# Three places for gathered rows and four for table tiles, instead of four and three, in a hybrid encoder's expert layer

## The chip, the cores and the metric

The kernel runs on one core of a Trainium2 chip. The metric is the device time of one execution in microseconds. It took 4031.67 us in the median of three runs, which lay between 4027.1 and 4036.65 us.

## What is computed

The program is a two-layer encoder trunk on 256 tokens of width 2048, all in float32. Each layer first mixes tokens in four parallel branches (a 2-D Fourier transform, a state space model, grouped-query attention and a bidirectional RWKV-7) and then applies an expert layer that looks up single-neuron experts by product keys. Only the expert layer is touched here:

```
q   = (xc @ w_query)                                  # 8 heads
s1, i1 = top_k(scores of half 1, 16);  s2, i2 = top_k(scores of half 2, 16)
top_s, pos = top_k(s1[:, None] + s2[None, :], 16)     # 16 of 256 candidates per token and head
idx  = i1 * 128 + i2 at pos                           # of 16384 experts
gate = softmax(top_s)
act  = gelu(sum_d expert_u[idx] * xc)
out  = sum over heads and picks of gate * act * expert_v[idx]
```

So each token uses 128 rows of `expert_u` and 128 rows of `expert_v`, each row 2048 numbers (8 KB) long.

## The kernel before, in words

Each of the two turns of the layer loop runs the mixers, the RWKV part, the output projection with the query projection (`route`), and then `experts`, which is the place of the change.

`experts` treats the tokens in two ways. 160 of them (`DENSE`) are computed densely: TensorE multiplies the whole tables with them, tile by tile. There are 128 tiles (`TILES`) of the transposed `peer_u` (this document calls them the u tiles), each [128, 2048] float32, that is 1 MB, and then 128 tiles of `peer_v` (the v tiles), also 1 MB each. A u tile costs 16 products into one bank (L1672), ScalarE applies the GELU to them (L1789, L1791) into `W`, and a v tile costs 16 products (L1745) that add up over all 128 tiles in six banks. The other 96 tokens are served sparsely: in three sets of 32 tokens, 32 steps for `peer_u` and 32 for `peer_v` each, 192 gathers in all (`ROWS_IN`). One gather brings one row for each of the 128 partitions (32 tokens by 4 picks), so again 1 MB, in two halves of 512 KB that GpSimd issues as two indirect DMAs (L1629). VectorE then takes it in `serve(n)`: a dot product for `peer_u` (L1935), a multiply-add into `sums` for `peer_v` (L1941).

Both streams have a ring of places in SBUF, and a place of either ring is 8 KB per partition. `ring` has `SLOTS` places for table tiles. SyncE issues tile i (L1593 for u, L1598 for v) when the products of tile i - SLOTS are done (semaphore `tile_mm`). The first `SLOTS` u tiles are issued without a wait, right behind the last piece of the query weights. `place` has `RING` places for gathered rows. GpSimd issues row n when VectorE has served row n - RING (semaphore `place_free`). The tiles go through the hardware queue q1, the gathers through the software queue q0; both use the same 16 DMA engines.

The order of VectorE's work is written out by hand. While TensorE goes through u tiles 0 to 61, VectorE looks for the best picks of the dense tokens (`find(0, h)`) and serves two rows after each head, and then serves on up to row 29. It then waits until u tile 60, since `exps(0)` stands there on ScalarE. From u tile 64 (`FIRST`) on it makes one-hot tables for the gates of four tokens per tile, multiplies gates into `W`, and serves 9 rows for every 10 tiles (`served`). TensorE makes the gates (L1681) ahead of tiles 64 to 103. With the v tiles VectorE has nothing but the remaining rows: it serves them as they come. TensorE puts a few small products among the tiles: `widen` (L1695) spreads a set's tokens for the dot products, `fold` (L1708) adds a set's sums up. After the last v tile TensorE folds the third set, which needs the sums of row 191, and transposes the dense results (L1761); VectorE adds both to `x` (L1950, L2009), and the layer is over.

In the following, four stages of `experts` are told apart. Their times in the second layer are: A1, u tiles 0 to 61 (2801 to 3086 us); A2, the u tiles with gates, 62 to 103 (3086 to 3302 us); A3, the remaining u tiles (3302 to 3419 us); V, the v tiles (3419 to 4012 us). In the first layer they begin at 787, 1072, 1288 and 1409 us, and V ends at about 2002 us.

Of the kernel before, what the change touches and what calls it, by code (L numbers as in the profile page):

```python
# [32 lines left out]
HALF_K = 8  # L33
WRING = 3
TILES = KEYS
SLOTS = 3
RING = 4
SET, SETS, STEPS = 32, 3, 32
DENSE = SEQ - SET * SETS
ROWS_IN = SETS * 2 * STEPS  # L40
# [81 lines left out]
def build(nc, t, out):  # L122
# [3 lines left out]
    with whole:  # L126
        first_sem = []

        def sem(name):
            s = whole.enter_context(nc.semaphore(name))  # L130
            first_sem.append(s)
            return s
# [35 lines left out]

        row_in = [sem(f"row_in{i}") for i in range(RING)]
        kept = len(first_sem)  # L170
# [1237 lines left out]
def query_piece(nc, t, layer, query, engine, h):  # L1408

    engine.dma_start(query["w"][:, h % WRING], t["peer_w_query"][layer][:, h * P:(h + 1) * P]  # L1410
                     .rearrange("(k p) n -> p k n", p=P)).then_inc(query["w_in"][h % WRING], 16)
# [118 lines left out]
def experts(nc, t, layer, sem, sb, bank, c, x, hT, query, W, low, layer_base, row_in):  # L1530
# [8 lines left out]
    rms_wide, rms_mm, h_scaled = sem("ex_rms_wide"), sem("ex_rms_mm"), sem("ex_h_scaled")  # L1539
    tile_in, tile_mm, tile_out = [sem(f"ex_tile_in{i}") for i in range(SLOTS)], sem("ex_tile_mm"), sem("ex_tile_out")  # L1540
    best_ready, exp_ready, picks_ready, picks_mm, picks_out = [sem("ex_" + n) for n in ("best", "exp", "picks", "picks_mm",
# [7 lines left out]
    with ExitStack() as st:  # L1549
# [3 lines left out]

        ring = sb(st, "ex_tile", [P, SLOTS, KT * P])
        place = sb(st, "ex_row", [P, RING, D])
        h_wide = sb(st, "ex_h_wide", [P, D])
# [30 lines left out]
        with nc.Block() as block:  # L1587
            @block.sync
            def _(sp):
                def u_tile(i, slot, free):  # L1590
                    if free is not None:
                        sp.wait_ge(tile_mm, free)
                    sp.dma_start(ring[:, slot, :], t["peer_uT"][layer, i].rearrange("p k e -> p (k e)"))\  # L1593
                        .then_inc(tile_in[slot], 16)
# [6 lines left out]
                for h in range(WRING, PEER_H):  # L1601
                    sp.wait_ge(q_mm, h - WRING + 1)
                    query_piece(nc, t, layer, query, sp, h)
                whole_laps = TILES // SLOTS
                for i in range(SLOTS):
                    u_tile(i, i, None)
                with sp.Fori(1, whole_laps) as lap:
                    for e in range(SLOTS):
                        u_tile(lap * SLOTS + e, e, lap * SLOTS + (e + 1 - SLOTS))
                for i in range(whole_laps * SLOTS, TILES):  # L1610
# [11 lines left out]
            def _(pool):  # L1622
                pool.wait_ge(rows_ready, SETS * 4 * 2)
                for n in range(ROWS_IN):
                    s, table, step = n // (2 * STEPS), n // STEPS % 2, n % STEPS
                    if n >= RING:
                        pool.wait_ge(place_free, n - RING + 1)
                    for half in range(2):
                        nc.gpsimd.indirect_dma_start(  # L1629
                            out=place[:, n % RING, half * D // 2:(half + 1) * D // 2], out_offset=None,  # L1630
                            in_=tables[table][:, :],
                            in_offset=bass.IndirectOffsetOnAxis(ap=rows[:, s, half, step:step + 1], axis=0))\
                            .then_inc(row_in[n % RING], 16)

# [400 lines left out]
```

## Time and profile before

| | us |
|---|---|
| median of three runs | 4031.67 |
| the profiled execution, its own time | 4039.34 |
| its span, first to last instruction | 4037.5 |
| TensorE busy in the span | 3754.7 |
| VectorE busy in the span | 2310.8 |
| GpSimd busy in the span | 977.3 |
| moved by the DMA engines | 1077.47 MB |

The profile is of one execution. Busy time is the union of an engine's instructions; issues of DMAs on SyncE are not counted as busy, while those of GpSimd (the indirect ones) are. "DMA share" in a window is the mean busy share of the 16 DMA engines; it can come out slightly above 1. In the chain of waits a piece "DMA" is the time from a DMA's issue to its landing, when that landing is what released the next piece.

### The profile page before, as it was taken

To read this page: it belongs to the slowest core of one execution; us is meant where nothing else is said; L and a number is where in the kernel's file an instruction comes from. 1 tells how busy PE (TensorE), PEld (TensorE's weight loads), DVE (VectorE), ACT (ScalarE), POOL (GpSimd) and SP (SyncE) were. 2 spreads that over 40 slices of the span, in tenths; PEclk is the share of its full clock that TensorE was granted. 3 is DMA by queue.
4 is the path that set the end of the run, shared out by engine and by line. 5 is a ranking of instruction groups with operands and counts; after the bars stand their busy time and mean duration, and the time that the engine had idled before them with its cause. 6 is when DMAs were issued, how large, how long until landed. Compare 5 with 4: busy or idle time off the path is not lost. (4 is left out here: it accounts for less than half of the span.)

```text
span 4037.5 us, 63918 instructions
## 1 busy us (share of the span) xinstructions
PE 3754.7 (93%) x26660; PEld 3402.6 (84%) x26660; DVE 2310.8 (57%) x4099; ACT 429.9 (11%) x1020; POOL 977.3 (24%) x868
## 2 busy tenths in 40 slices
PE   6997889999999999999869978899999999999997
PEld 5776774899999999999857867748999999999997
DVE  6975752695287534344469757527952875444444
ACT  1013220100111000000010132101001110000000
POOL 2510000034033333333226100000340333333331
PEclk9998899999999999999989988999999999999999
DMA  5340014399799999999744300153997999999997
GB/s 155 117 133 10 1 43 155 123 358 402 277 381 381 414 416 414 415 412 415 317 127 132 118 10 1 43 161 126 369 409 282 380 386 412 415 415 415 412 414 305
DMA packets 334771, 1077.47 MB, mean 267 GB/s; under 512 B 52197, under 2 KB 150873, under 8 KB 268441
## 3 DMA queue, kind: packets, MB, share of 16 engines
q1 hardware_dynamic: 223896, 670.72, 43.8%
q0 software_dynamic: 110592, 402.70, 25.2%
q8 instruction: 212, 3.47, 0.4%
q14 instruction: 71, 0.57, 0.0%
HBM read 1071.23 MB, written 2.10 MB: 266 GB/s over the span
## 5 line engine op out<-in xcount | busy, mean ns | idle before, releaser
L1745 PE MATMUL bank<-ex_W,ex_tile 128*128 128x160 f32 x8192 | 1132.6, 300 | 39.1 <-DMA ex_tile<-in_peer_v 38.8
L1745 PEld LDWEIGHTS bank<-ex_W,ex_tile 128*128 128x128 f32 x8192 | 1114.9, 190 | 60.3 <-DMA ex_tile<-in_peer_v 52.9
L1672 PE MATMUL bank<-ycT,ex_tile 128*128 128x160 f32 x8192 | 1142.8, 300 | 24.0 <-DMA ex_tile<-in_peer_uT 21.7
L1672 PEld LDWEIGHTS bank<-ycT,ex_tile 128*128 128x128 f32 x8192 | 1119.3, 190 | 39.9 <-DMA ex_tile<-in_peer_uT 30.5
L1629 POOL DMA_INDIRECT ex_row<-in_peer_u,ex_rows x384 | 404.1, 1052 | 1850.9 <-DVE ex_rows L1905 1188.7
L1941 DVE SCALAR_TENSOR_TENSOR ex_sums<-ex_row,ex_weight,ex_sums 128x2048 f32<-128x2048 f32 x186 | 437.0, 2349 | 411.4 <-DMA ex_row<-in_peer_v,ex_rows 362.3
L1935 DVE CUSTOM_DVE_ANT_0 ex_row<-ex_row,ex_h_wide 128x2048 f32<-128x2048 f32 x192 | 438.7, 2290 | 366.7 <-DMA ex_row<-in_peer_u,ex_rows 288.9
L1629 POOL DMA_INDIRECT ex_row<-in_peer_v,ex_rows x384 | 364.7, 950 | 890.2 <-DVE ex_sums L1941 560.5
L359 PE MATMUL pj_bank<-pj_hT,pj_piece 128*128 128x256 f32 x2048 | 459.5, 383 | 5.9 <-DVE pj_hT L632 3.6
L359 PEld LDWEIGHTS pj_bank<-pj_hT,pj_piece 128*128 128x128 f32 x2048 | 388.4, 192 | 72.0 <-issue 13.8
L824 PE MATMUL bank<-arena,ycT 128*128 128x512 f32 x512 | 222.4, 593 | 2.0 <-PEq L909 2.0
L824 PEld LDWEIGHTS bank<-arena,ycT 128*128 128x128 f32 x512 | 96.6, 190 | 121.4 <-issue 121.2
L994 PE MATMUL bank<-arena 128*128 128x128 f32 x1152 | 140.9, 283 | 7.6 <-DVE arena L1342 7.5
L994 PEld LDWEIGHTS bank<-arena 128*128 128x128 f32 x1152 | 136.7, 198 | 10.3 <-issue 10.1
L1993 DVE TENSOR_TENSOR ex_W<-ex_W,ex_gelu 128x160 f32<-128x160 f32 (+26 forms) x128 | 35.2, 275 | 174.7 <-ACT ex_gelu L1789 97.2
L1417 PE MATMUL bank<-ycT,query_w 128*128 128x256 f32 x512 | 114.9, 382 | 2.0 <-PEq L1434 2.0
L1791 ACT ACTIVATE ex_W<-bank 128x160 f32<-128x160 f32 (+20 forms) x206 | 57.0, 277 | 525.1 <-PE bank L1672 480.3
L1417 PEld LDWEIGHTS bank<-ycT,query_w 128*128 128x128 f32 x512 | 95.8, 190 | 16.5 <-issue 2.7
L1919 DVE TENSOR_SCALAR ex_hot<-consts,ex_picksT 128x128 f32<-128x128 f32 x320 | 109.5, 342 | 0.0
L1516 DVE TENSOR_TENSOR x<-bank,x 128x512 f32<-128x512 f32 x16 | 11.1, 692 | 168.3 <-PE bank L824 168.1
L1918 DVE TENSOR_SCALAR ex_hot<-consts,ex_picksT 128x128 f32<-128x128 f32 x320 | 90.2, 282 | 15.4 <-ACT ex_picksT L1823 15.4
L605 POOL TENSOR_TENSOR s_table<-s_factor 128x1024 f32<-128x1024 f32 x16 | 32.6, 2035 | 273.8 <-DVE s_factor L710 151.2
(375 smaller groups left out, 3129.3 us busy)
## 6 DMA issues: line engine op xcount, KB each, us to landing
ex_tile<-in_peer_uT SPq DMA_DIRECT2D x256, 1024.0 KB
ex_tile<-in_peer_v SPq DMA_DIRECT2D x256, 1024.0 KB
pj_piece<-in_w_in SPq DMA_DIRECT2D x32, 2048.0 KB, 8.8
arena<-in_w_out SPq DMA_DIRECT2D x16, 2048.0 KB, 8.2
query_w<-in_peer_w_query SPq DMA_DIRECT2D x16, 1024.0 KB, 6.0
ex_row<-in_peer_u,ex_rows POOLq DMA_INDIRECT x384
ex_row<-in_peer_v,ex_rows POOLq DMA_INDIRECT x384
x<-in_x SPq DMA_DIRECT2D x1, 2048.0 KB, 8.8
```

What stands on the lines that cost most here:

```text
L359: mm = mmul(pj_bank[:, n % 2, m * SEQ:m * SEQ + SEQ], piece[:, n % 2, k, m * P:m * P + P], hT[:, k, :], start=(m == 0 and k == 0), stop=(k ...
L824: mm = nc.tensor.matmul(bank[:, out_bank(n) + b, :], ycT[:, kh * HALF_K + k, b * P:b * P + P], out_w["place"][:, i % 2, k, :], start=(kh = ...
L994: mm = mmul(bank[:, b, j * P:j * P + P], left[:, d, j, :], right[:, d, j, :], start=(j == 0), stop=True, skip_group_check=True)
L1417: mm = nc.tensor.matmul(bank[:, h % 2, 0:SEQ], query["w"][:, h % WRING, k, :], hT[k // 4][:, k % 4, :], start=(k == 0), stop=(k == KT - 1) ...
L1629: nc.gpsimd.indirect_dma_start(out=place[:, n % RING, half * D // 2:(half + 1) * D // 2], out_offset=None, in_=tables[table][:, :], in_off ...
L1672: mm = mmul(o, ring[:, j % SLOTS, k * P:k * P + P], hT[k // 4][:, k % 4, 0:DENSE], start=(k == 0), stop=(k == KT - 1))
L1745: mm = mmul(bank[:, at_, lo:lo + DENSE], ring[:, i % SLOTS, m * P:m * P + P], W[:, j, :], start=(j == 0 and m % 3 == 0), stop=(j == TILES ...
L1791: last = A.activation(W[:, j, n:DENSE], a[:, n:DENSE], ACT.Gelu)
L1918: V.tensor_scalar(hot2[:, g % 2, i, :], c("iota"), picksT[:, 1, n:n + 1], None, ALU.is_equal)
L1919: mm = V.tensor_scalar(hot1[:, g % 2, i, :], c("iota"), picksT[:, 0, n:n + 1], picksT[:, 2, n:n + 1], ALU.is_equal, ALU.mult)
L1935: V.tensor_tensor_reduce(out=row, in0=row, in1=h_wide[:], scale=1.0, scalar=0.0, op0=ALU.mult, op1=ALU.add, accum_out=dot[:, step:step + 1 ...
L1941: V.scalar_tensor_tensor(sums[:], row, weight[:, step:step + 1], sums[:], ALU.mult, ALU.add)\
```

## The change

Two constants are exchanged. `SLOTS` becomes 4 and `RING` 3. All else follows from them: the places of the two rings (`ring` and `place`), the number of their semaphores, the waits that free a place (`i - SLOTS`, `n - RING`), and the way SyncE's two loops over the tiles are split into whole turns and a rest. With `SLOTS` = 4 the loops come out even: 128 tiles are 32 turns of four.

```diff
--- before.py
+++ after.py
@@ -33,8 +33,8 @@
 HALF_K = 8
 WRING = 3
 TILES = KEYS
-SLOTS = 3
-RING = 4
+SLOTS = 4
+RING = 3
 SET, SETS, STEPS = 32, 3, 32
 DENSE = SEQ - SET * SETS
 ROWS_IN = SETS * 2 * STEPS
```

## Rows read from the trace of the kernel before

**Rows 1.** The page: DMA share and GB/s in 40 slices, then the two queues

```profile
DMA  5340014399799999999744300153997999999997
GB/s 155 117 133 10 1 43 155 123 358 402 277 381 381 414 416 414 415 412 415 317 127 132 118 10 1 43 161 126 369 409 282 380 386 412 415 415 415 412 414 305
q1 hardware_dynamic: 223896, 670.72, 43.8%
q0 software_dynamic: 110592, 402.70, 25.2%
```

**Rows 2.** Busy times by stretch: stages of layer two, three stretches inside, V of layer one

```profile
core 0: us, PE busy (x) PEld busy (x) DVE busy (x) ACT busy (x) POOL busy (x), PEclk, DMA share, GB/s
2801.00:3086.00 285.00, 275.57 (x2011) 272.51 (x2011) 172.06 (x461) 31.07 (x79) 83.26 (x68) 1.00 0.90 351
3086.00:3302.00 216.00, 216.00 (x1648) 215.68 (x1648) 173.56 (x434) 31.81 (x129) 62.32 (x67) 1.00 0.92 355
3302.00:3419.00 117.00, 114.76 (x812) 109.53 (x812) 60.45 (x75) 7.83 (x27) 43.27 (x45) 1.00 1.02 411
3419.00:4012.00 593.00, 571.72 (x4127) 560.02 (x4125) 248.44 (x155) 8.06 (x17) 193.97 (x206) 1.00 1.01 410
...
3033.00:3086.00 53.00, 52.69 (x387) 52.45 (x387) 0.78 (x3) 6.45 (x15) 0.00 (x0) 1.00 0.77 286
3640.00:3780.00 140.00, 135.13 (x981) 133.20 (x980) 55.37 (x45) 0.00 (x0) 46.01 (x49) 1.00 1.02 415
```

**Rows 3.** TensorE's waits for tiles: A1, A3, V, each layer one and then two

```profile
PE bank L1672 <- DMA ex_tile<-in_peer_uT: 9.2, 10, 3.9
...
PE bank L1672 <- DMA ex_tile<-in_peer_uT: 8.1, 8, 3.1
...
PE bank L1672 <- DMA ex_tile<-in_peer_uT: 2.4, 4, 1.1
...
PE bank L1672 <- DMA ex_tile<-in_peer_uT: 2.0, 3, 0.9
...
PE bank L1745 <- DMA ex_tile<-in_peer_v: 19.7, 30, 1.1
...
PE bank L1745 <- DMA ex_tile<-in_peer_v: 19.1, 27, 1.2
```

**Rows 4.** Chain of waits in A1: start us, us, what

```profile
2882.86 9.47 DMA ex_tile<-in_peer_uT
2892.34 0.04 issue
2892.38 8.97 PE bank L1672 x64
```

**Rows 5.** Chain of waits in V, one turn of a row's place, and a shorter flight

```profile
3760.57 19.46 DMA ex_row<-in_peer_u,ex_rows
...
3780.06 2.29 DVE ex_row L1935
3782.35 0.02 DVE ex_dot L1935
3782.37 0.26 issue
3782.63 0.94 POOL ex_row L1629
3783.56 0.30 issue
...
3810.60 14.73 DMA ex_row<-in_peer_u,ex_rows
```

**Rows 6.** Timeline at the end of V: last tiles, last rows, then fold

```profile
3989.59 22.00 PE L1745 MATMUL bank<-ex_W,ex_tile 128*128 128x160 f32 x160 [0.89 <-DMA ex_tile<-in_peer_v]
...
4007.05 4.84 DVE L1941 SCALAR_TENSOR_TENSOR ex_sums<-ex_row,ex_weight,ex_sums 128x2048 f32<-128x2048 f32 x2 [2.89 <-DMA ex_row<-in_peer_v,ex_rows]
...
4012.00 3.80 PE L1708 MATMUL bank<-ex_sums,consts 128*32 128x512 f32 x8 [0.41 <-DVEq L1945]
```

**Rows 7.** Timeline of VectorE: row 29 served, and the wait for ScalarE behind it

```profile
3025.23 2.29 DVE L1935 CUSTOM_DVE_ANT_0 ex_row<-ex_row,ex_h_wide 128x2048 f32<-128x2048 f32 x1 [4.29 <-DMA ex_row<-in_peer_u,ex_rows]
...
3079.04 0.29 DVE L1890 TENSOR_REDUCE ex_total<-ex_picks 128x8 f32<-128x128 f32 x1 [51.50 <-ACT ex_picks L1796]
```

**Rows 8.** The page: a 1 MB load while no other stream runs, us to landing

```profile
query_w<-in_peer_w_query SPq DMA_DIRECT2D x16, 1024.0 KB, 6.0
```

## The prediction

> **What bounds the kernel now.** I read the slices of the page first: outside `experts` the DMA engines are half idle, inside it they are nearly always full at about 415 GB/s, and their two queues move two thirds of all bytes there [rows 1]. Then the windows by stage [rows 2]. In A1 TensorE is busy 275.6 of 285 us and the DMA engines 0.90; in A2 TensorE is busy all the time (its products alone set the pace) at 355 GB/s; in A3 and V the DMA engines are full (1.02 and 1.01) and TensorE loses 2 and 21 us. Third, who TensorE waits for: table tiles, 8 to 9 us in A1, 2 us in A3 and some 20 us in V in each layer [rows 3]. Last, the end of V [rows 6]: the last tile's products end at 3989.6 + 22.0 = 4011.6 us and the last row is served at 4007.05 + 4.84 = 4011.9 us. The two streams end together, and the fold behind them needs both. So V is bound by the volume that both streams put through the same 16 engines: 593 us at 410 GB/s are 243 MB, that is 232 pieces of 1.049 MB, which is about 128 tiles and the 105 rows that are left of 192 (87 are served by u tile 127, by `served`).
>
> That is the main point. **A place given to the other stream adds no bandwidth.** It can only win where the DMA engines have room now, and it can lose where one stream alone must fill them.
>
> **Where room exists, A1.** TensorE waits there for tiles though the mean load is 0.90. A tile is issued when the tile three before it is done, so it has two tiles' time, 8.97 us (the x64 are two tiles) [rows 4], and took 9.47 us. With four places it has three tiles' time, about 13.3 us. The longest wait is 3.9 us [rows 3], which is below the added 4.4 us. So all tile waits of A1 go: 9.2 + 8.1 = 17.3 us, 8.65 per layer. They are on the path: TensorE is what sets A1's length, and A2 behind it is TensorE's alone. What could be late next is VectorE with one row place fewer. Its row 29 is served at 3027.5 us, and then it waits 51.5 us for ScalarE [rows 7]. The 30 rows could each be 1.7 us later before that is used up. I cost it at nothing. The volume moved ahead in that pause is unchanged: the rings hold four tiles and three rows then instead of three and four. The pause runs at 286 GB/s in 53 us [rows 2], and it is what the 8.65 us are taken from.
>
> **A2.** No tile waits now, none after. A row is due every 5.24 us (a tile with its gates; 216 us for 40 such tiles and two without gates comes to about that). With three places a turn has 15.7 us. Of a turn, serving, release and first issue take 2.29 + 0.02 + 0.26 + 0.94 + 0.30 = 3.8 us [rows 5], so the flight may take 11.9 us. The trace does not show flights there, since none is waited for. In V, with the engines full, they take 14.7 to 19.5 us [rows 5], but most of that is queueing behind the stream's own other rows: 593 us for 105 rows are 5.65 us a row, and four places turn in 22.6 us. At 355 GB/s there is room, so I cost A2 at nothing; the third rival has it otherwise.
>
> **A3 and V, the tiles.** Here the 20 and 2 us of waits hang on the same rule, flight against two or three tiles' time. The longest wait is 1.2 us [rows 3], well inside the added 4.4. TensorE's V is then 571.7 us instead of 593 [rows 2], and with A1 and A3 its last tile ends 8.65 + 2.2 + 20.5 = about 31.4 us earlier in each layer. These 22.7 us of A3 and V are no gain in themselves, because the rows are not there.
>
> Whether the tiles can take more of the engines than now is the open step. The trace has both shares while both streams wait: 135.1 us of TensorE's 140 are busy, that is 30.6 tiles, and 49 half rows in the same 140 us [rows 2]. That is 229 GB/s for tiles and 184 for rows. A table tile goes as 8 KB packets and a row as 4 KB ones (402.70 MB in 110592 packets are 3.6 KB in the mean, the small ones are completions [rows 1]; a partition's share of a tile is 8 KB). The Trainium skill, page "DMA: Bandwidth & Descriptors", section on arbitration, says that an engine goes round robin between its queues, a packet at a time. By that rule two queues that are both never empty would share 2:1, 277 and 138 GB/s; the trace's 229 and 184 are between that and halves. If the rule holds, the tile queue is empty part of the time, and one more tile in flight fills it; if it does not, the shares stay. The sum below takes neither figure.
>
> I take it that the waits go, since TensorE cannot take more than a tile per 4.41 us: 238 GB/s. The rows then get 415 - 238 = 177 GB/s, 5.92 us a row instead of 5.65, and they are behind when the tiles are through.
>
> **The tail of V.** The last tile landed at about 4007.2 us (22.0 us of five tiles, less one, from 3989.6). After the change it lands 31.4 us earlier and another 4.4 us ahead of its use, about 3971. The last row is landed at about 4009.5 us now, and with the engines full throughout it would be 8.65 us earlier, 4000.8. So 29.5 us of full engines are left for rows alone: 29.5 x 415 / 1.049 = 11.7 rows. They must go through three places. A turn is 3.8 us plus the flight of a half row on free engines. The nearest row is the 1 MB load without a rival, 6.0 us [rows 8]; half of its bytes less (0.5 MB at 415 GB/s, 1.26 us) gives 4.7. (3.8 + 4.7) / 3 = 2.9 us a row, against 2.53 at full engines. 11.7 x 2.9 = 33.9 us, and the row stream ends at 4005.1, 4.3 us earlier than now. The bounds: VectorE with the release takes 2.6 us a row, which gives 30.4 us and 7.8 us earlier; a flight as long as that of a loaded tile, 9.47 us [rows 4], gives 4.4 us a row, 51.5 us and 13 us later. I take 2.9, because nothing competes in the tail. The fold and what follows it wait for the rows alone, as now.
>
> **Loss of fill.** With one row fewer in flight the engines might run empty between. A3 speaks against it: VectorE is paced by the tiles there, so rows often lie landed in their places, and the engines are still at 1.02 [rows 2]. Nothing for the sum.
>
> **Sum.** 4.3 us per layer, 8.6 us in all: 4039.3 of the profiled execution becomes 4030.7. The median of the runs is 0.19% below that execution, and in the same ratio I get 4031.7 - 8.6 = 4023 us. The bounds of the tail alone make it 4016 to 4058.
>
> **Rivals.**
> 1. *The shares are fixed by the queues.* Then a fourth place does nothing in A3 and V, tiles and rows end together as before, and A1's 17.3 us are all kept: 4014 us. For it: tiles fly over 9 us in A1 and in V alike. Against it: where TensorE is slower for the folds, the row flight falls to 14.7 us [rows 5], so the rows take what the tiles leave.
> 2. *Nothing moves.* If the tiles' flight grows with one more in the queue (their share being fixed already in A1), the waits of A1 stay too: 4032 us.
> 3. *The rows starve, the slower side.* Three places bear the forecast's 5.92 us a row as long as the flight is under 3 x 5.92 - 3.8 = 14 us; this is the deciding point. If it does not fall below the shortest one seen, 14.7 us, a row takes 6.2 us. While the tiles run (563 us) 91 rows are served instead of 95, four more are left for the tail at 2.9 us: 12 us per layer worse than the forecast, 7.5 us worse than now, 4047 us. The same flight breaks A2's 11.9 us: 6.2 x 0.9 = 5.6 us a tile against 5.24, up to 13.6 us over 40 tiles, of which VectorE's pauses (173.6 of 216 us busy [rows 2]) take part: up to 4074. Were the flight to stay at 18.7 us, a row would take 7.5 us and the time would pass 4130; but that needs the flight not to depend on the rows in front, which the four-place turn speaks against.
>
> **How the numbers follow.** Forecast 0.55, rival 1 0.15, rival 2 0.10, rival 3 0.20. A measurement of this kernel can tell about 0.2%, 8 us, from no change; the forecast's 8.6 us are on that edge, so of its 0.55 I put 0.29 to faster, 0.20 to the same and 0.06 to slower (a long tail). Faster: 0.29 + 0.15 = 0.44. Same: 0.20 + 0.10 = 0.30. Slower: 0.06 + 0.20 = 0.26. The range reaches from below rival 1 to the middle of rival 3: 4009 to 4062 us. The forecast's own is 4016 to 4040.
>
> **What the profile after would show.** TensorE's waits for tiles in A1 gone (they were 17.3 us) and A2 starting 8 to 10 us earlier in each layer; in V TensorE at about 572 us, waiting at its end some 20 us or more for row 191, with rows alone on the engines in the last 30 us at under 415 GB/s; row flights of about 14 us in V. If instead tile waits of 20 us remain in V and both ends coincide, rival 1 was right. If VectorE waits for rows in A2, or TensorE waits there at all, it is rival 3. The prediction is wrong above all if the tail runs slower than 3.3 us a row, or if the rows lose more than 0.27 us each while the tiles run.

## The result

The changed kernel took 4059.09 us in the median of four runs (4052.73 to 4061.04), the kernel before 4032.7 us in four (4027.1 to 4036.65). The ratio is 1.0063, 95% interval 1.0048 to 1.0078: 0.63% slower, some 26 us, where 9 us less was forecast. The range of 4009 to 4062 us holds it, on its slower side. The profiled executions stand at 4060.33 against 4039.34 us, 21 us apart. Of the eleven executions of the last experiment's kernel, two took 8860.52 and 6779.49 us; no comparison below counts them.

The page of the changed kernel, its slices first (DMA share and GB/s, 40 slices), to be read beside [rows 1]:

```profile
DMA  5340015499899999999644300154998999999996
GB/s 154 117 133 10 1 43 161 135 369 409 320 379 389 408 416 414 413 376 416 251 126 135 115 9 2 43 161 152 378 411 320 381 390 399 416 413 415 371 416 256
```

In V of both layers there are now two holes: slices of 376 and 371 GB/s in the middle, and last slices of 251 and 256, where the kernel before had 412 to 416 throughout and last slices of 317 and 305 [rows 1].

TensorE's waits, all of the execution that concern `experts`:

```profile
PE bank L1708 <- DVE x L1950: 56.3, 4, 24.5
PE bank L1708 <- DVEq L1945: 47.2, 2, 24.8
```

No wait for a tile is left, in any stage; those of [rows 3] are gone. In their place TensorE waits for VectorE, and so for the rows, at the folds (L1708): 103.5 us in the two layers.

Windows of layer two (A1, A3, V as a whole; then V cut into four parts, and two pieces of the second part; columns as in [rows 2]):

```profile
2809.00:3081.00 272.00, 272.00 (x2009) 271.74 (x2009) 171.91 (x461) 30.76 (x78) 75.23 (x66) 1.00 0.92 363
...
3297.00:3417.00 120.00, 115.73 (x818) 110.83 (x817) 58.77 (x73) 7.89 (x27) 40.06 (x43) 0.99 1.01 400
3417.00:4031.00 614.00, 565.00 (x4122) 559.85 (x4120) 250.50 (x157) 8.16 (x17) 215.57 (x210) 0.96 0.99 396
3417.00:3786.00 369.00, 369.00 (x2708) 366.98 (x2707) 141.31 (x92) 4.94 (x10) 114.63 (x123) 1.00 1.02 414
3786.00:3811.00 25.00, 0.50 (x5) 0.29 (x4) 14.49 (x13) 0.00 (x0) 16.15 (x12) 0.60 0.84 299
3811.00:3997.00 186.00, 186.00 (x1344) 183.33 (x1345) 73.72 (x43) 0.23 (x1) 63.36 (x64) 0.99 1.01 407
3997.00:4031.00 34.00, 9.49 (x70) 9.25 (x69) 20.98 (x9) 2.99 (x6) 21.43 (x12) 0.68 0.64 215
...
3786.00:3795.00 9.00, 0.47 (x4) 0.22 (x2) 4.18 (x3) 0.00 (x0) 3.07 (x4) 0.78 1.00 404
3795.00:3811.00 16.00, 0.04 (x1) 0.07 (x2) 10.31 (x11) 0.00 (x0) 13.08 (x8) 0.50 0.75 240
```

While both streams run, TensorE is busy without a gap and the engines move 414 GB/s. Then TensorE stands still for 25 us. By the times of the packets, tiles already under way still land in the first 8 of them; from 3795 on the rows are alone and bring 240 GB/s. In the last window the tiles are through, and the rows bring 215. Measured at 415 GB/s, the two windows lack 25 x (1 - 299/415) + 34 x (1 - 215/415) = 7.0 + 16.4 = 23.4 us.

The same reckoning holds for the layer: time x (1 - rate/415), before and after, is 44.0 and 34.1 us in A1, 31.2 in A2 both times, 1.1 and 4.3 in A3, 7.1 and 28.1 in V. The sum grew by 14.3 us; layer two as a whole, up to the first transpose, grew by 14.0.

The stages in us (layer one, layer two), cut in both traces at the first u tile, the first L1720, the last gate product (L1681), the first v tile and the first transpose:

| | A1 | A2 | A3 | V, up to the first transpose |
|---|---|---|---|---|
| before | 288.1, 283.9 | 216.9, 216.9 | 117.1, 117.0 | 596.0, 596.2 |
| changed | 271.3, 271.4 | 216.9, 216.9 | 117.3, 119.3 | 617.4, 620.4 |

A1 gained 29.3 us in the two layers, V lost 45.6, A3 2.5. That is 18.8 of the 21 us, very unevenly split: 4.8 us in layer one, 14.0 in layer two.

The timeline of TensorE in the changed kernel shows where it stood still:

```profile
3777.50 8.96 PE L1745 MATMUL bank<-ex_W,ex_tile 128*128 128x160 f32 x64
3810.96 1.89 PE L1708 MATMUL bank<-ex_sums,consts 128*32 128x512 f32 x2 [24.50 <-DVE x L1950]
...
4031.29 6.32 PE L1708 MATMUL bank<-ex_sums,consts 128*32 128x512 f32 x8 [24.79 <-DVEq L1945]
```

The first is the third of the four folds of set two: it reuses a bank, so it needs the first one's addition to `x`, and VectorE makes that addition only at row 152. The rows were late, the tiles early. The second is the end of V. The fold behind that wait also ran slower: 6.32 us against 3.80 [rows 6]. The granted clock was 0.50 from 3795 to 3811, that is the lower of the two levels (1.2 and 2.4 GHz), after TensorE had stood still; 0.60 and 0.68 are means over windows in which it changed. At the end of the layer this costs 2.5 us (2.2 in layer one, 5.98 us against 3.80).

### The profile page after: what moved, and what is told of

Same layout as the page of the kernel before. It is cut to its first block and busy times, and to the rows that moved or that the text cites. A ratio compares the mean times of both kernels' runs of the same rounds, so it can differ in the third digit from the quotient of the medians.

```text
span 4058.5 us, 63890 instructions
## 1 busy us (share of the span) xinstructions
PE 3741.4 (92%) x26660; PEld 3405.4 (84%) x26660; DVE 2312.0 (57%) x4099; ACT 429.5 (11%) x1020; POOL 995.6 (25%) x868
## 5 line engine op out<-in xcount | busy, mean ns | idle before, releaser
L1672 PE MATMUL bank<-ycT,ex_tile 128*128 128x160 f32 x8192 | 1131.2, 299 | 0.0
L1745 PE MATMUL bank<-ex_W,ex_tile 128*128 128x160 f32 x8192 | 1118.9, 300 | 0.0
L1629 POOL DMA_INDIRECT ex_row<-in_peer_v,ex_rows x384 | 381.4, 993 | 856.6 <-DVE ex_sums L1941 588.8
L1708 PE MATMUL bank<-ex_sums,consts 128*32 128x512 f32 x48 | 31.5, 772 | 103.5 <-DVE x L1950 56.3
L1417 PEld LDWEIGHTS bank<-ycT,query_w 128*128 128x128 f32 x512 | 95.8, 190 | 16.5 <-issue 2.7
L1919 DVE TENSOR_SCALAR ex_hot<-consts,ex_picksT 128x128 f32<-128x128 f32 x320 | 109.2, 341 | 0.0
L1708 PEld LDWEIGHTS bank<-ex_sums,consts 128*32 128x32 f32 x48 | 4.6, 126 | 115.0 <-issue 67.3
```

What stands on the lines that cost most here:

```text
L1417: mm = nc.tensor.matmul(bank[:, h % 2, 0:SEQ], query["w"][:, h % WRING, k, :], hT[k // 4][:, k % 4, :], start=(k == 0), stop=(k == KT - 1) ...
L1629: nc.gpsimd.indirect_dma_start(out=place[:, n % RING, half * D // 2:(half + 1) * D // 2], out_offset=None, in_=tables[table][:, :], in_off ...
L1672: mm = mmul(o, ring[:, j % SLOTS, k * P:k * P + P], hT[k // 4][:, k % 4, 0:DENSE], start=(k == 0), stop=(k == KT - 1))
L1745: mm = mmul(bank[:, at_, lo:lo + DENSE], ring[:, i % SLOTS, m * P:m * P + P], W[:, j, :], start=(j == 0 and m % 3 == 0), stop=(j == TILES ...
L1919: mm = V.tensor_scalar(hot1[:, g % 2, i, :], c("iota"), picksT[:, 0, n:n + 1], picksT[:, 2, n:n + 1], ALU.is_equal, ALU.mult)
```

## The experiments

The theory formed from this result is called T in the expectations: each stream is paced by its own needs as long as both run, and the engines are full; the fourth tile place takes away the tiles' waits, so the tiles run ahead, and twice per layer the rows are left alone, where they can't fill the engines. Its rival R: three places starve the rows whatever the tiles do.

**Three and three.** `SLOTS = 3`, `RING = 3`:

```diff
-SLOTS = 4
+SLOTS = 3
 RING = 3
```

> Three places for tiles and three for rows: the row place is given up, the tile place is not added. Theory T (what costs is that the tiles no longer wait, run ahead of the rows and leave the rows alone on the engines, at the fold of set two and in the tail): with three tile places TensorE waits for tiles in V again (some 20 us a layer), no stall at L1708 for x, no long tail; V 593 to 600 us, in all 4030 to 4042 us. Rival R (three row places alone starve the rows): V as in the changed kernel, 610 us or more, in all 4060 us or more, since A1's gain is missing too.

Measured: 4049.61 us in the median of ten against 4043.33 for the kernel before on the same chip, ratio 1.0014 (1.0004 to 1.0023). TensorE waits for tiles in V again (32.1 us in both layers), V lasts 603.6 and 604.8 us. At the end of V TensorE waits 9.5 and 11.6 us for the rows. Both sides missed: V is longer than T's 593 to 600 us and shorter than R's 610. So R holds a part: one row place fewer costs V 8 us per layer here, and 2.5 us in the next experiment, of the 23 us that the changed kernel lost there. With A3, which the next experiment lengthened too, it is 8 to 9 us against 4 to 7. It is not the cause of the whole. Part of it is again the clock: the last fold takes 6.37 us here and 5.40 us there, instead of 3.80, after waits of 9.5 and 4.7 us.

**The v tiles issued one tile later.** The changed kernel with four places for u tiles, and in V the wait of three:

```diff
                 def v_tile(i, slot, free):
-                    sp.wait_ge(tile_mm, free)
+                    sp.wait_ge(tile_mm, free + 1)
```

> The changed kernel, but each v tile is issued one tile later, as with three places; the u tiles keep four. Theory T: V goes back to 593 to 600 us, A1's gain stays: 4012 to 4026 us. Rival R (three row places are the cause): V stays above 610 us, 4055 us or more.

Measured: 4026.76 against 4043.33 us, ratio 0.9961 (0.9945 to 0.9978): 16.6 us faster than the kernel before. With the same three row places as the changed kernel, V is 598.3 and 598.9 us instead of 617.4 and 620.4. TensorE's waits:

```profile
PE bank L1745 <- DMA ex_tile<-in_peer_v: 32.8, 50, 1.2
PE bank L1708 <- DVE x L1950: 8.6, 2, 5.1
PE bank L1708 <- DVEq L1945: 7.9, 2, 4.7
```

TensorE waits for tiles 33 us again, and only 16.5 us at the folds instead of 103.5. T holds against R for the larger part of the loss: a wait that looked like the loss was what kept the two streams in step.

**Later folds.** In the changed kernel the folds of set two stand ten tiles later and their additions three rows later:

```diff
-WIDEN_2, FOLD_1, FOLD_1_AT = 36, 80, 152
+WIDEN_2, FOLD_1, FOLD_1_AT = 36, 90, 155
```

> The changed kernel with the folds of set two among the v tiles ten tiles later and their additions three rows later, so that TensorE need not wait there. Theory T: the stall of 24.5 us at L1708 moves to the end of V, where the rows are alone for longer; 4050 to 4062 us. Rival F (the order of the folds itself is the cause): the stall goes and does not come back: 24 us less per layer, about 4010 us.

Measured: 4057.61 against 4043.33 us, ratio 1.0035 (1.0025 to 1.0046), while the changed kernel's 1.0063 came from another chip. So both were run again on one chip.

> The changed kernel once more, so that it stands on one chip beside the one with later folds: 22 to 30 us slower than the kernel before by every theory; its profile the same stall at the fold of set two and the same tail.

> The folds of set two later, once more beside the changed kernel. Theory T: the time that TensorE waits for the rows is moved, not saved, within 5 us of the changed kernel. If the first comparison (ratio 1.0035 where the changed kernel had 1.0063) was real, 8 to 14 us faster than the changed kernel: then part of the stall is work for which the engines had room.

Measured on one chip, with 4030.54 us before: the changed kernel 4056.31 us, ratio 1.0057 (1.0040 to 1.0074); later folds 4052.61 us, ratio 1.0062 (1.0045 to 1.0080). The two can't be told apart, and the 1.0035 of the first comparison did not come again; why it was lower stays open. TensorE's waits with later folds:

```profile
PE bank L1708 <- DVEq L1945: 74.2, 2, 38.0
PE bank L1708 <- DVE x L1950: 24.5, 4, 9.7
```

98.7 us against 102.3 in the changed kernel on the same chip (53.3 and 49.0): the wait went from the fold of set two to the end of V. The order of the folds is not the cause; it only decides where the rows are alone.

**The rows alone.** How fast they go then was the disputed term. The kernel before and the changed one, each with v tiles cut to 64 bytes per partition:

```diff
-sp.dma_start(ring[:, slot, :], ...[layer, i])
+sp.dma_start(ring[:, slot, 0:16], ...[layer, i, :, 0:16])
```

> The kernel before (three tile places, four row places), but of each v tile only 64 bytes per partition are loaded (left out: the rest of the v tiles, so the dense tokens' result is not that of the reference). The rows have the DMA engines to themselves in V. Theory P (a lone row's pace is set by GpSimd's two issues, held up while VectorE works on a row): about 4 us a row, POOL's issues often over 2 us. Rival L (the pace is the flight over the number of places): with four places 2.6 to 3.0 us a row.

> The same cut in the changed kernel (four tile places, three row places). Theory P: the same pace as with four row places, about 4 us. Rival L: a third slower than with four places, 3.5 to 4 us against 2.6 to 3.

The same 100 us in each, within V of layer two (3430 to 3530): GpSimd's issues and what they waited for (count, busy us, mean ns, idle us), four row places first, then three:

```profile
L1629 POOL DMA_INDIRECT ex_row<-in_peer_v,ex_rows x50 | 87.7, 1753 | 15.2 <-issue 15.2
```

```profile
L1629 POOL DMA_INDIRECT ex_row<-in_peer_v,ex_rows x48 | 84.2, 1754 | 14.6 <-issue 14.6
L1629 POOL DMA_INDIRECT ex_row<-in_peer_u,ex_rows x2 | 3.6, 1798 | 0.6 <-issue 0.6
```

50 half rows in 100 us either way: 4.0 us a row, at 259 and 258 GB/s, whatever the number of places. In this stretch GpSimd never waits for a place; it issues all the time, and an issue takes 1.75 us in the mean, where it takes 0.94 in V of the kernel before [rows 5]. Rival L is refuted. A few lines of its timeline in the kernel with four row places:

```profile
3508.49 0.94 POOL L1629 DMA_INDIRECT ex_row<-in_peer_v,ex_rows  x1 [0.30 <-issue]
3508.87 2.35 DVE L1941 SCALAR_TENSOR_TENSOR ex_sums<-ex_row,ex_weight,ex_sums 128x2048 f32<-128x2048 f32 x1 [1.49 <-DMA ex_row<-in_peer_v,ex_rows]
3509.74 2.30 POOL L1629 DMA_INDIRECT ex_row<-in_peer_v,ex_rows  x1 [0.30 <-issue]
3512.34 0.94 POOL L1629 DMA_INDIRECT ex_row<-in_peer_v,ex_rows  x1 [0.30 <-issue]
```

VectorE's operation ends at 3511.22 and the long issue at 3512.04: the issue began during the operation and ended 0.8 us after it. That VectorE holds it up was told apart from a full queue by shortening VectorE's operation to a quarter of its columns:

```diff
-V.scalar_tensor_tensor(sums[:], row, weight[:, step:step + 1], sums[:], ALU.mult, ALU.add)
+V.scalar_tensor_tensor(sums[:, 0:512], row[:, 0:512], weight[:, step:step + 1], sums[:, 0:512], ALU.mult, ALU.add)
```

(and the dot product likewise).

> The kernel with the rows alone on the engines in V and four row places (v tiles cut to 64 bytes per partition), and now VectorE's operation on a served row takes only 512 of its 2048 columns (left out: the other columns of both operations; the gathers are unchanged). Theory P (GpSimd's issue is held up while VectorE works on a row): the issues over 2 us shrink with VectorE's operation, to about 1.2 us and less; GpSimd then needs 1.24 us per half, 2.5 us a row, and the rows go at 2.5 to 2.9 us each. Rival Q (GpSimd waits because its queue is full): the faster the rows are taken the more it would wait; its long issues stay over 2 us and the pace at about 4 us.

The two groups on GpSimd and the one on VectorE in the same stretch:

```profile
L1629 POOL DMA_INDIRECT ex_row<-in_peer_v,ex_rows x39 | 38.8, 994 | 14.2 <-issue 13.4 <-DVE ex_sums L1941 0.7
L1629 POOL DMA_INDIRECT ex_row<-in_peer_u,ex_rows x8 | 7.8, 979 | 2.4 <-issue 2.4
```

```profile
L1941 DVE SCALAR_TENSOR_TENSOR ex_sums<-ex_row,ex_weight,ex_sums 128x512 f32<-128x512 f32 x23 | 17.3, 752 | 43.9 <-DMA ex_row<-in_peer_v,ex_rows 43.9
```

The issue fell to 0.99 us in the mean, and VectorE starts a row each 2.6 us (3481.22, 3483.82, 3486.45, 3489.00). That the same 100 us hold fewer issues than before (47 against 50) has another reason, which the windows show:

```profile
3470.00:3492.00 22.00, 22.00 (x164) 22.00 (x163) 6.01 (x8) 0.00 (x0) 16.93 (x17) 1.00 1.04 403
3492.00:3530.00 38.00, 38.00 (x282) 38.00 (x281) 0.00 (x0) 0.00 (x0) 0.94 (x1) 1.00 0.17 60
```

VectorE is through with a set's rows at 3490 and waits for TensorE to spread the next set's tokens, and the places fill up; until then they alone fill the engines, at 403 GB/s, where they brought 259 before. Theory P holds, Q is refuted: GpSimd issued back to back all that time, and its issues were short. The Trainium skill, page "SBUF — State Buffer", section "SBUF: two separate sides", says that GpSimd and VectorE share a pair of ports, and that a VectorE operation holds it for its whole length in a two-port mode, or when it has two inputs in SBUF and the GpSimd operation reads SBUF. Of the issue of a DMA it says so only for the two-port modes. The two operations here have two inputs in SBUF and the issue reads its row numbers from there, so 1.75 against 0.99 us agrees with the rule for two inputs; that the port is the cause no run here shows.

**Whole rows.** The changed kernel with one gather of 8 KB per partition in place of two of 4 KB:

```diff
-tables = [t[n].rearrange("l e (h d) -> (l e h) d", h=2) for n in ("peer_u", "peer_v")]
+tables = [t[n].rearrange("l e d -> (l e) d") for n in ("peer_u", "peer_v")]
...
-                    for half in range(2):
+                    for half in range(1):
```

> The changed kernel with one gather of whole 8 KB rows in the place of two of 4 KB halves. Theory P: GpSimd issues once per row, so rows alone go at under 3.5 us and the tail of V shrinks; and if the engines take turns packet by packet, rows of 8 KB get as much as the tiles while both queue, up to 207 GB/s, so that the rows keep up, the stall at the fold goes and TensorE waits for tiles again: 4015 to 4035 us. If the shares do not depend on the packets and GpSimd's issue sets nothing: 4059 us as the changed kernel.

Measured: 4079.95 against 4041.44 us, ratio 1.0090 (1.0074 to 1.0106), slower than either side had it. Whether rows alone then go at under 3.5 us did not show, since here they never had to go alone. But the shares came out as expected. TensorE's tiles and VectorE's rows in V:

```profile
3605.37 4.61 PE L1745 MATMUL bank<-ex_W,ex_tile 128*128 128x160 f32 x32 [0.35 <-DMA ex_tile<-in_peer_v]
...
3610.34 4.61 PE L1745 MATMUL bank<-ex_W,ex_tile 128*128 128x160 f32 x32 [0.36 <-DMA ex_tile<-in_peer_v]
```

```profile
3604.79 2.35 DVE L1941 SCALAR_TENSOR_TENSOR ex_sums<-ex_row,ex_weight,ex_sums 128x2048 f32<-128x2048 f32 x1 [3.04 <-DMA ex_row<-in_peer_v,ex_rows]
3609.76 2.35 DVE L1941 SCALAR_TENSOR_TENSOR ex_sums<-ex_row,ex_weight,ex_sums 128x2048 f32<-128x2048 f32 x1 [2.62 <-DMA ex_row<-in_peer_v,ex_rows]
```

A tile each 4.97 us and a row each 4.97 us: equal packets, equal halves, 211 GB/s each. Now the rows are ahead, and VectorE waits for TensorE's folds, in the middle of V and at its end (V of layer two):

```profile
DVE x L1950 <- PE bank L1708: 112.8, 6, 66.0
...
4058.95 0.70 DVE L1950 TENSOR_TENSOR x<-bank,x 32x512 f32<-32x512 f32 x1 [34.03 <-PE bank L1708]
```

In both places the tiles are left alone, and they can't bring more than TensorE's 238 GB/s: V is 627.7 and 626.7 us. The hole is the same with the streams exchanged. The time I gave (4015 to 4035) had left out that halves are too much for 105 rows beside 128 tiles.

**A place that changes hands.** If the fourth tile place is worth 29 us with the u tiles and nothing with the v tiles, it should go to the rows for V. Rows below 90 use three places; from row 93 on the fourth tile place is the rows' fourth, once u tile 127 is done; the v tiles turn in three:

```diff
+    if n < SWAP:                       # SWAP = 90
+        return n % 3, n // 3
+    k = (n - SWAP) % 4
+    return k, (SWAP // 3 if k < 3 else 0) + (n - SWAP) // 4
...
+        places = [place3[:, 0, :], place3[:, 1, :], place3[:, 2, :], ring[:, 3, :]]
...
+                    if n == SWAP + 3:
+                        pool.wait_ge(tile_mm, TILES)
```

> Four tile places and three row places while the u tiles run; from row 93 on the fourth tile place belongs to the rows, so V has three tile places and four row places as in the kernel before. Theory T: A1's gain of about 17 us with V as before: 4012 to 4018 us. Rival R says the same of V; if A1's gain were lost again behind it (rows behind at the start of V), 4030 us.

> The kernel in which the fourth tile place goes to the rows from row 93 on, with more rounds and for its profile. Theory T: A1 without tile waits, V with the two ends within a few us of each other and tile waits of about 20 us a layer; 17 to 24 us faster than before. Rival (the gain is given back behind A1): V longer than 598 us and less than 8 us gained.

Measured: ratio 0.9934 (0.9917 to 0.9950) in the first and 0.9940 (0.9924 to 0.9955) in the second, against 4043.33 and 4041.44 us before: 24 to 27 us faster, at or above what was expected (14 to 20, then 17 to 24), since A1 is worth more than the 17 us of its listed waits. The trace is of the second. A1 is 271.4 and 271.8 us, V 598.3 and 596.9. The end of V, as in [rows 6]:

```profile
3973.72 4.61 PE L1762 MATMUL bank<-ex_W,ex_tile 128*128 128x160 f32 x32 [0.75 <-DMA ex_tile<-in_peer_v]
...
3975.38 4.84 DVE L1959 SCALAR_TENSOR_TENSOR ex_sums<-ex_row,ex_weight,ex_sums 128x2048 f32<-128x2048 f32 x2
...
3980.33 3.80 PE L1725 MATMUL bank<-ex_sums,consts 128*32 128x512 f32 x8 [2.00 <-DVEq L1963]
```

The streams end at 3978.3 and 3980.2 us, the fold takes 3.80 us again. This version beats both kernels.

## Why the prediction was wrong

The step that failed is the pace of the rows when they are alone, put at 2.9 us and measured at 4.0, because GpSimd's issues and not the flights set it. The parts in turn:

- *What bounds V* was right: the volume of both streams, as long as both run. 369 us at 414 GB/s in the changed kernel say the same.
- *A1* was right in kind and too small. All tile waits went, and A1 is 29.3 us shorter in the two layers, not 17.3. The idle time that the rows of waits list is not all that a wait costs. The two tiles behind a wait take 8.97 us [rows 4], and in the changed kernel the chain has 57 tiles in a row:

```profile
2833.26 247.76 PE bank L1672 x1824
```

4.347 us each, 8.69 for two. So each stop costs 0.28 us beside its idle time, and A1 had 18 of them for tiles and 4 others: 6 us of the 12 that I had missed, with 2 us more listed as "issue". Most of the other 4 us is one place in layer one of the kernel before, behind the longest wait:

```profile
842.74 37.53 PE L1672 MATMUL bank<-ycT,ex_tile 128*128 128x160 f32 x253 [3.92 <-DMA ex_tile<-in_peer_uT]
...
838.00:860.00 22.00, 18.08 (x116) 17.84 (x115) 20.80 (x68) 1.22 (x4) 9.37 (x8) 0.84 0.97 376
```

253 of these take 34.4 us at the pace of the long piece (1824 in 247.76 us), so 3.2 us went to the clock, which stood at 0.84 in the mean there. In the changed kernel the same 113 us from 787 on have a clock of 1.00, against 0.97 before.
- *A2* at nothing was right: 216.9 us in all four cases. VectorE had no wait for a row there. A row was also due there more seldom than I had it, one per 5.8 us and not per 5.24, as 9 rows go with 10 tiles. *A3* became 2.5 us longer in the two layers, though its tile waits of 4.4 us went: TensorE waited 3.7 and 4.3 us at its fold.
- *The tiles' waits in V go*, the step called open: right, not one is left. They were worth more than the 20.5 us listed: with the v tiles cut to 64 bytes, so that TensorE waits for none, V is 566.6 us against 596, 29.5 us less. The rows at 5.92 us: they took 6.0 (123 halves in 369 us), 0.35 us more than before, so the sign that I had set at 0.27 came true by a little. Their flights, 14.2 to 20.6 us in the chain of V before, fell to 14 us in the median, as in these pieces of the changed kernel's chain:

```profile
3908.71 14.03 DMA ex_row<-in_peer_v,ex_rows
...
3926.63 15.10 DMA ex_row<-in_peer_v,ex_rows
```

  So rival 1 was wrong, and rival 3 in its form too: A2 held, and at 6.0 us instead of 5.92 the rows are about one behind the forecast when the tiles are through, not four. In the changed kernel the tiles take the 238 GB/s that TensorE can use and the rows get 174; with 8 KB rows against 8 KB tiles the shares are equal. Both agree with the rule of turns by packet, which the prediction took from the Trainium skill, page "DMA: Bandwidth & Descriptors"; its 277 and 138 GB/s for two queues that are never empty no run here shows.
- *The folds* were a part that I did not cost at all. TensorE's fold of set two waits for row 152. With tiles earlier and rows later, 24.5 us of the tiles' lead were spent there. By the runs with later folds this costs nothing that can be measured by itself; it moves part of the rows' time alone from the tail to the middle.
- *The tail* is the step that failed. I put a lone row at (3.8 + 4.7) / 3 = 2.9 us, flight over places (the quotient is 2.8). The flight was not what was most off (the gathers of the changed kernel's last 34 us, from the line's own view):

```profile
DMA to landing us min/median/max: 5.0/6.0/6.8
```

  With 6.0 us the same rule gives 3.3 us a row. But a row takes 4.0 us there (VectorE starts the last six from 4008.63 to 4028.82) as in the kernels with the rows alone, because GpSimd's issues are the limit: two per row, one of them mostly held up by VectorE's operation. In V of the kernel before this hardly shows, as GpSimd issues while VectorE waits for a row; there an issue takes 0.94 us in the median. It does show in A1, where VectorE serves two rows in a run and the first of them frees a place (duration in ns, min/median/max):

```profile
L1629 POOL DMA_INDIRECT ex_row<-in_peer_u,ex_rows x64: 937/941/2967, 2836.9 to 3017.4; - x64
```

  Ten of the 68 issues of A1 in layer two took over 2 us. I had taken the 0.94 us of [rows 5] for every issue, and had not asked whether the issues could be the limit. The bound of 4.4 us was wide enough, the reason for it was another. With 4.0 us the 11.7 rows take 47 us instead of 34, and the layer's 4.3 us of gain become 9 us of loss; with A1's further 6 us per layer taken in, 3 us of loss. The slower last folds are 2.2 to 2.5 us per layer more, and the 407 GB/s of the stretch behind the stall lack 186 x (1 - 407/415) = 3.6 us. That makes 9 us, and the mean of the two layers is 9.4; but the layers are 4.8 and 14.0 us, so this close a fit is in part luck. It is an account of the profiled executions, which are 21 us apart, and not of the medians, which are 26 us apart.
- *Loss of fill at nothing*: nearly right while the tiles press, as in the first 369 us; three row places beside three tile places in use cost V 2.5 to 8 us per layer, and 4 to 9 us with A3, by the first two experiments.

## What to carry to other kernels

Where two streams share full DMA engines, a buffer place moves bandwidth from one to the other, and what counts is whether both end together; the wait of one stream for its data may be the thing that keeps them so. Price the stretch in which one stream is left alone by its flight over its places and also by what issues it, and take the larger. And look for every point at which the one stream waits for the other in the middle, since a lead is spent there.

## What the runs showed of the hardware

- The issue of a gather of 128 half rows by GpSimd takes 0.94 us while VectorE waits, and up to 3.04 us while VectorE works on rows of 2048 float32 columns with two operands in SBUF; in the mean 1.75 us where GpSimd issues without a pause, 0.99 us when VectorE's operation is cut from 2.35 to 0.75 us.
- Tiles in 8 KB packets against rows in 8 KB packets split the engines evenly, 4.97 us for each 1 MB piece of either; against rows in 4 KB packets the tiles get all that TensorE can use (238 GB/s) with four tile places and three row places, and 229 GB/s with three and four.
- After TensorE had stood still for 24.8 us, a fold of eight products took 6.32 instead of 3.80 us; after 4.7 us it took 5.40. While it stood still its granted clock was 0.50 (3795 to 3811).
- By the profile's times, each stop of TensorE before a tile costs 0.28 us beside the idle time listed (8.97 against 8.69 us for two tiles).
